# Mixture of experts: expert 0 with 64 unsplit places first, the three fullest other experts split, four more buffers for the first tiles

## The reference

```python
def moe_ffn(h, router_w, w1, w3, w2):
    logits = (h @ router_w).astype(jnp.float32)
    top_vals, top_idx = lax.top_k(logits, TOP_K)          # TOP_K = 2
    top_w = jax.nn.softmax(top_vals, axis=-1)
    gate = jnp.sum(jax.nn.one_hot(top_idx, N_EXPERTS, dtype=jnp.float32) * top_w[..., None], axis=-2)
    out = jnp.zeros_like(h)
    for e in range(N_EXPERTS):
        out = out + gate[..., e:e + 1].astype(h.dtype) * swiglu(h, w1[e], w3[e], w2[e])
    return out
```

## Time and profile before

| | |
|---|---|
| median of 3 runs | 2225.95 us (2222.59 to 2227.03) |
| the profiled execution, its own time | 2226.49 us |
| its span | 2224.7 us |
| TensorE matmul busy | 2108.1 us (95% of the span) |
| TensorE weight load busy | 1787.5 us (80%) |
| VectorE busy | 1347.3 us (61%) |
| ScalarE busy | 1010.9 us (45%) |
| DMA, mean over the span | 220 GB/s, 489.49 MB |
| the 264 expert tiles | issued in two groups of 132, median 13.4 and 14.6 us from issue to landing |

### The profile page before, as it was taken

One profiled execution on the slowest core, in us unless ns is written; L12 is line 12 of the kernel. 1 busy time (PEld: TensorE's weight loads), 2 busy tenths in 40 slices (PEclk: granted clock), 3 DMA queues, 4 the chain that ended last, 5 costly groups with the idle time before them and its releaser, 6 DMA issues. The chain is left out here.

```text
span 2224.7 us, 38921 instructions
## 1 busy us (share of the span) xinstructions
PE 2108.1 (95%) x15459; PEld 1787.5 (80%) x15459; DVE 1347.3 (61%) x2453; ACT 1010.9 (45%) x1759; POOL 124.2 (6%) x115
## 2 busy tenths in 40 slices
PE   8999999999989999989999999889999999998998
PEld 7988889998978888889999888888875568555774
DVE  5565667466668676877666675876941177213942
ACT  5545545546545444456344353455731065113731
POOL 0100000000000050030000041030000000000000
PEclk9999999999999999999999999998999999999999
DMA  6443334444346453354554443356999999999996
GB/s 198 143 136 95 96 114 146 140 140 142 103 123 171 144 155 102 105 179 156 201 194 135 133 152 114 96 171 279 365 361 420 421 420 410 410 420 421 421 396 274
DMA packets 257819, 489.49 MB, mean 220 GB/s; under 512 B 35256, under 2 KB 208216, under 8 KB 223720
## 3 DMA queue, kind: packets, MB, share of 16 engines
q1 hardware_dynamic: 252112, 484.39, 60.4%
q0 software_dynamic: 656, 1.80, 0.2%
q10 hardware_dynamic: 4872, 0.81, 0.2%
HBM read 485.91 MB, written 1.05 MB: 219 GB/s over the span
## 5 line engine op out<-in xcount | busy, mean ns | idle before, releaser
L1336 PE MATMUL bank<-memr 128*128 128x256 f32 (+3 forms) x7056 | 899.7, 287 | 37.6 <-DVE memr L2392 9.6
L1336 PEld LDWEIGHTS bank<-memr 128*128 128x128 f32 (+2 forms) x7056 | 858.4, 186 | 68.9 <-issue 21.0
L2392 DVE TENSOR_TENSOR memr<-mem_low,memr 128x1024 fp32r<-128x1024 f32 (+3 forms) x328 | 398.0, 1232 | 62.9 <-ACT memr L1842 62.2
L1842 ACT CAST memr<-mem_low 128x1024 fp32r<-128x1024 f32 (+3 forms) x328 | 333.3, 1032 | 118.6 <-PE bank L1336 115.6
L1035 ACT ACTIVATE mem_high<-bank 128x128 f32<-128x128 f32 (+1 forms) x88 | 27.9, 317 | 306.2 <-PE bank L854 261.7
L1232 DVE SCALAR_TENSOR_TENSOR mem_high<-mem_high,bank 128x128 f32<-128x128 f32 (+1 forms) x88 | 29.4, 335 | 225.4 <-ACT mem_high L1035 225.4
L847 PE MATMUL bank<-memr 128*128 128x512 f32 x400 | 134.9, 406 | 9.9 <-DVE memr_tail L1178 9.9
L656 PE MATMUL bank<-memr 128*128 128x256 f32 x960 | 117.1, 283 | 3.1 <-DVE memr L2411 3.1
L656 PEld LDWEIGHTS bank<-memr 128*128 128x128 f32 x960 | 115.8, 191 | 3.5 <-issue 3.5
L1178 DVE TENSOR_TENSOR memr_tail<-mem_tail,memr 128x2048 fp32r<-128x2048 f32 x42 | 95.4, 2287 | 32.3 <-ACT memr L1002 31.8
L854 PE MATMUL bank<-mem_ring,mem_low 128*64 128x256 f32 x896 | 102.7, 381 | 1.1 <-DMA mem_ring<-in_moe 1.1
(11 more groups left out here) (357 smaller groups left out, 3018.6 us busy)
## 6 DMA issues: line engine op xcount, KB each, us to landing
mem_tail<-in_moe SPq DMA_DIRECT2D x132, 1024.0 KB, 13.4
mem_ring<-in_moe SPq DMA_DIRECT2D x132, 1024.0 KB, 14.6
mem_low<-in_w_in SPq DMA_DIRECT2D x112, 1024.0 KB, 5.1
mem_tail<-in_ffn_w SPq DMA_DIRECT2D x18, 1024.0 KB, 8.3
mem_low<-in_w_out SPq DMA_DIRECT2D x16, 1024.0 KB, 5.3
mem_low<-in_w_branch SPq DMA_DIRECT2D x12, 1024.0 KB, 5.0
mem_high<-in_ffn_w SPq DMA_DIRECT2D x12, 1024.0 KB, 8.0
mem_low<-in_w_branch SPq DMA_DIRECT2D x16, 512.0 KB, 3.5
```

What stands on the lines that cost most here:

```text
L1336: ins = pe.matmul(out(bank), lhsT, rhs, start=((k, i) == order[0] and not half), stop=((k, i) == order[-1]), skip_group_check=half is not ...
L1842: cp(high, raw).then_inc(*sig("w_high", i))
L2392: st(V.tensor_tensor(low, raw, high, ALU.subtract), sig("w_split", i))
```

## The change

Expert 0 (rank 0) gets 64 places and is not split; ranks 1, 2 and 3 get 128 and are split; ranks 4 to 7 have 64. The order becomes light, light, heavy, light, heavy, light, heavy, light: still three heavy and five light experts. The four high-part buffers are not needed while expert 0 and the next expert run, so they take raw tiles 12 to 15 first; `FIRST` is 16 tiles that can be loaded ahead. TensorE allows these four by a count of `HI` when the router's choice is known, right before the sums that place the tokens. ScalarE's first split waits until tile 15 has been used. Since rank 0 has other room than ranks 1 and 2, up to four passes are possible and VectorE computes the number with four more small operations.

```diff
-ROOMS = [2 * GROUP] * HEAVY + [GROUP] * (EXPERTS - HEAVY)
-TURN = [0, 3, 4, 1, 5, 6, 2, 7]
+ROOMS = [2 * GROUP if 0 < r <= HEAVY else GROUP for r in range(EXPERTS)]
+TURN = [0, 4, 1, 5, 2, 6, 3, 7]
+FIRST = RAW + HI
...
+        raw_hi, hi_r = map(list, zip(*[carve_both(2048) for _ in range(3)]))
+        raw += raw_hi
+        hi_f = [v.bitcast(F32) for v in hi_r]
         hi_f.append(memr_squares[:, 0:2048].bitcast(F32))
         hi_r.append(memr_squares[:, 0:2048])
+        raw.append(sq.rearrange("p a b -> p (a b)")[:, 0:2048])
...
         def tile_done(p, n):

-            return family("m_done"), p * TILES + n + 1 + RAW
+            return family("m_done"), p * (TILES + FIRST) + n + 1 + FIRST
...
+        def slot_of(n):
+
+            return n if n < FIRST else (n - FIRST) % RAW
...
             pe.wait_ge(*at("chosen"))
+            pe.sem_inc(family("m_done"), HI)
...
-                    sp.wait_ge(family("m_done"), p * TILES + n + 1)
+                    if n < FIRST:
+                        sp.wait_ge(family("m_done"), p * (TILES + FIRST) + n + 1)
+                    else:
+                        sp.wait_ge(*tile_done(p, n - (FIRST if n < FIRST + RAW else RAW)))
...
-                if at_ >= HI:
-                    act.wait_ge(*tile_done(p, SPLIT[at_ - HI]))
-                cp(hi_r[at_ % HI], raw[n % RAW]).then_inc(family("m_high"), 1)
+                act.wait_ge(*tile_done(p, SPLIT[at_ - HI] if at_ >= HI else FIRST - 1))
+                cp(hi_r[at_ % HI], raw[slot_of(n)]).then_inc(family("m_high"), 1)
...
+                    if s == 0:
+                        expert_in(p, 0)
                     if s < UPS and heavy(i):
                         high(p, up_tile(s, 0))
                         high(p, up_tile(s, 1))
-                        if s == 0:
-                            expert_in(p, 0)
```

More of the change, by code:

```diff
@@ L63 @@
 TILE_ORDER.update({down_tile(g): (g, 2) for g in range(UPS)})
-SPLIT = [n for n in range(TILES) if TURN[TILE_ORDER[n][0] // HALF] < HEAVY]
+SPLIT = [n for n in range(TILES) if ROOMS[TURN[TILE_ORDER[n][0] // HALF]] > GROUP]
 def constants():
@@ L326, in build @@
         top[0] = 0
-        assert len(raw) == RAW
-        hi_f, hi_r = map(list, zip(*[high_places(2048) for _ in range(3)]))
+        assert len(raw_r) == RAW
+        raw_hi, hi_r = map(list, zip(*[carve_both(2048) for _ in range(3)]))
+        raw += raw_hi
+        hi_f = [v.bitcast(F32) for v in hi_r]
         hi_f.append(memr_squares[:, 0:2048].bitcast(F32))
         hi_r.append(memr_squares[:, 0:2048])
+        raw.append(sq.rearrange("p a b -> p (a b)")[:, 0:2048])
         assert len(hi_r) == HI
@@ L744, in heavy @@
         def heavy(i):
-            return TURN[i] < HEAVY
+            return ROOMS[TURN[i]] > GROUP
         def parts(i):
@@ L754, in heavy_before @@
             return sum(heavy(k) for k in range(i))
+        def slot_of(n):
+            return n if n < FIRST else (n - FIRST) % RAW
         def raw_loaded(p, n):
-            return family(f"m_raw{n % RAW}"), p * (16 * TILES // RAW) + 16 * (n // RAW + 1)
+            k = slot_of(n)
+            if k >= RAW:
+                last = max(range(k - RAW, len(chunks), NSLOT))
+                s, before = at(f"w_loaded{k - RAW}", last)
+                return s, p * 16 + before + 16
+            loads = len(range(k, TILES - FIRST, RAW)) + 1
+            return family(f"m_raw{k}"), p * 16 * loads + 16 * (1 if n < FIRST else (n - FIRST) // RAW + 2)
         def split_done(p, n):
@@ L842, in up @@
                         pe.wait_ge(*split_done(p, n))
-                        high, low = hi_r[SPLIT.index(n) % HI], raw_r[n % RAW]
+                        high, low = hi_r[SPLIT.index(n) % HI], raw_r[slot_of(n)]
                         for k in range(4):
@@ L888, in down @@
                             ins = pe.matmul(SB[0][64 * half:64 * half + 64, :], act_t[:, d % 2, GROUP * f:GROUP * (f + 1)],
-                                            raw[n % RAW][:, f * D + 512 * half:f * D + 512 * half + 512],
+                                            raw[slot_of(n)][:, f * D + 512 * half:f * D + 512 * half + 512],
                                             start=(c == 0 and f == 0), stop=(c == HALF - 1 and f == 1),
@@ L954, in body @@
                 pe.wait_ge(family("m_out_gained"), p * 4 + 4)
+                pe.sem_inc(family("m_done"), FIRST)
             turns(pe, body)
@@ L1158, in moe_dve @@
             st(V.tensor_reduce(most[:, 1:2], over2, AX.X, ALU.max))
+            st(TTn(over3, over2, const("room"), ALU.subtract))
             st(TS(most[:, 2:3], most[:, 0:1], 0.5, 1.0, ALU.is_gt, ALU.add))
@@ L1171, in moe_dve @@
             st.settle()
-            assert PASSES == 3
+            assert PASSES == 4
             def low(p, n):
@@ L1177, in low, with expert_in @@
                 dve.wait_ge(family("m_high"), p * len(SPLIT) + at_ + 1)
-                TTn(raw_r[n % RAW], raw[n % RAW], hi_f[at_ % HI], ALU.subtract).then_inc(family("m_split"), 1)
-            def expert_in(p, i, halves=(0, 1)):
+                TTn(raw_r[slot_of(n)], raw[slot_of(n)], hi_f[at_ % HI], ALU.subtract).then_inc(family("m_split"), 1)
+            def expert_in(p, i):
                 if heavy(i):
-                    for j in halves:
+                    for j in range(2):
                         dve.wait_ge(family("m_he_high"), p * 2 * HEAVY + 2 * heavy_before(i) + j + 1)
```

19 lines of the change are left out of this document (10 added, 9 removed).

## The result

| | before | changed |
|---|---|---|
| median of 5 runs each, side by side | 2227.03 us (2222.59 to 2231.88) | 2211.26 us (2208.24 to 2212.32) |
| ratio | | 0.9929, 95% interval 0.9915 to 0.9943 |
| the profiled execution, its own time; span | 2226.49; 2224.7 us | 2209.96; 2208.1 us |
| TensorE matmul busy | 2108.1 us | 2103.8 us |
| first piece of the opening gather to the last marker | 673.58 us | 658.74 us |

The change is faster by 0.7%, 15.8 us by the medians (13 to 19 by the interval). The forecast was 21.4 us, a median of 2204.6 us.

A forecast was written before the change was run, and what follows sets the result against it. TensorE bounds the heavy experts, losing time between them to late tiles. Start 1541.5 plus eight expert lengths puts the last marker at 2186.8 instead of 2208.15: 21.4 us less, median 2204.6; main range 2201 to 2208, whole 2200 to 2215.

The forecast's parts named there:

- rival A: Stream not ahead at the first heavy expert, extra loads starting only at first tile use: 9.8 us back, 2214.4; chance 0.13.
- a stream without a pause: Sign of being right: DMA at about 420 GB/s without a pause from 1504 to 1700.
- no wait before any heavy expert: Sign of being right: no TensorE idle time over 1 us before any heavy expert's first split product.
- What bounds the kernel: TensorE bounds the heavy experts; a late tile load costs 3.85 us idle plus 1.63 of slow clock, 5.5 us per hole.
- A heavy expert without hole 99.7 us, light after heavy 73.0, light after light 68.8, last light 69.2: Expert lengths from marker to marker; heavy is 105.2 less 5.5, light after light is 72.14 measured less 3.3 of waits.
- The start, 1541.5 and 62.2 us: First product of the expert stage starts at about 1541.5; the first expert, now light, takes 62.2 us.
- I take neither: At the start, up to 1.6 us lost by clock and up to 1.5 us won by a faster 64-column gather, both left out.
- The stream: Four early loads remove the tile stream's pause at 1534.7; it never stops, and the 65th tile lands at 1666.7.
- 2.2 us of room: Before the first heavy expert: its first tile lands at 1666.7 and is needed by 1668.9, the forecast's tightest place.
- Rival B: Splitting, not loading, makes the hole: 5.5 us at each light-to-heavy change, only 4.9 us gained, 2221.1; chance 0.06.
- Rival C: The tile stream becomes the bound: slower under 395 GB/s mean, some 70 us slower at 358 GB/s; chance 0.02.
- Rival D: Expert 0 has more than 64 tokens, so the whole stage runs twice: some 2860 us; chance 0.01.

The follow-up runs named there:

- the two other orders: Changed kernel with light and heavy alternating from expert 0, two light experts adjacent at the end (2215.57 us, 0.9941) or in the middle (2215.64 us, 0.9949).
- the wide gather: Changed kernel with an opening gather of 128 columns instead of 64, the second 64 an unread copy: 2206.28 us (0.9900), again 2209.33 us (0.9915).
- the four loads late: Changed kernel with the four extra loads allowed only when TensorE is about to start its first product: 2215.87 us, 0.9944.
- the one with the seven products: Changed kernel with the 128-column opening gather plus seven unread matmuls, five before the router's choice and two before the gather: 2205.92 us, 0.9905.
- the two kernels kept busy: Changed kernel plus seven unread matmuls before the opening gather's end: with 64 columns 2208.42 us (0.9916), with 128 columns 2205.92 us (0.9905).

## Why the prediction was right, and what it missed

The sign was right, and so was the mechanism of the gain: the hole is a late tile, and the order and the four loads take most of it out. The size was off: 2211.26 us lies inside the whole range of 2200 to 2215, but above the main forecast of 2201 to 2208, in the band 2208 to 2215 to which rival A's 0.13 belonged, and two of its signs of being right (a stream without a pause, no wait before any heavy expert) did not hold. By its own steps:

- *What bounds the kernel.* Right. TensorE bounds the heavy experts, the load is behind the hole and not the split: shown by the two other orders (99.6 us and no wait for a heavy expert behind a single light one, 3.85 us behind a pair).
- *A heavy expert without hole 99.7 us, light after heavy 73.0, light after light 68.8, last light 69.2.* Measured 99.67 and 99.50, 73.08 and 73.09, 68.58, 69.16.
- *The start, 1541.5 and 62.2 us, "I take neither".* Here the two terms were mis-sized, by 3.7 us together. The forecast treated 64 and 128 columns as the same and gave a fall of the clock at most 1.6 us, the price of the old hole. Measured: the clock stayed at half through the whole gather and most of the first product; 0.77 us in the gather, 2.96 us in the first expert. The earlier trace rows had the warning: 0.50 and 0.69 at the old start, too. That the columns are the cause is shown by the wide gather: 62.23 and 62.24 us, the forecast's term; in three traces of it the first product took 3.67 us, in five of the narrow one 6.15 to 6.59.
- *The stream, "so the stream runs on", "it never stops", 2.2 us of room.* This step failed. The four loads did fill the old stop, but the first used buffer came free 11.4 us after the gather's start (1544.25) instead of 8.8 (1543.4), because of the slow first product, with 3.5 us lost, and at the 29th tile the distance of reuse falls from sixteen to twelve tiles, with 2.1 us lost. The second could have been read from the code: the condition in the diff that waits n - FIRST first and n - RAW after. In the first run of the wide gather both dents nearly vanish and the 65th tile is 4.5 us earlier after the gather's start; in the second it is 3.85 us earlier, with 328 and 390 GB/s from 1544 to 1560. Counted from the first load of the stage (1503.14 before, 1501.69 here) the tile was 171.3 - 163.6 = 7.7 us late. The dents explain 5.6 of it, and the rest is a term that the forecast put at nothing: it let the 65th tile land when 65 tiles' bytes had been moved, 68.16 MB. By 1673 the queues had moved 0.97 MB more (the DMA row of the first heavy expert), 2.3 us at 422 GB/s.
- *Rival A* in its mild form happened: "small losses of the stream give anything between". Its full form, the four loads late, came out near its number, 663.4 us where 652.2 + 9.8 = 662.0, but with 3.4 us lost at the start in it, which A had not counted.
- *Rival B* is refuted, by seven split heavy experts without a hole: five in the two other orders, and the second and third of the changed kernel. The one hole that came back there had the landing tile in front of it.
- *Rival C* did not happen: 421 GB/s over the 68 us from 1600, far above its 395. The Trainium skill (DMA: Bandwidth & Descriptors, section Bandwidth) states its share of about 358 GB/s for a core whose neighbour streams too. This program ran on one core, so the condition was not met and the 70 us of the prediction did not follow from it; no row here shows such a share.
- *Rival D*: there was one pass, not two.

Wait, clock and dents add up: 21.4 - 0.8 - 3.0 - 3.1 + 0.3 = 14.8 us in the trace; the medians say 15.8.

The best kernel seen by the traces is the changed one with the opening gather of 128 columns: 0.9900 and 0.9915 of the time before, 654.9 and 654.8 us for the stage (the timed runs do not tell it from the one with the seven products, 0.9905). What remains are 3 to 4 us at the first heavy expert (a wait of 1.7 to 2.3 us and what follows it). To get them the 65th tile has to land earlier, so either loads start earlier in the stage before or another buffer is found; neither was tried.

## What to carry to other kernels

Where a stream feeds two kinds of work, one faster than the stream and one slower, the order decides where its lead is eaten: put two fast pieces together only where the lead is largest, and count the buffers tile by tile at every change of the reuse distance, not only at the first. When a forecast takes out a wait at a phase's start, look up the granted clock there and ask what gives it back; after a pause a wider product can be the faster one. And once one wait is set by a transfer, work won ahead of it goes into the wait, and can lose the clock on top.

## What the runs showed of the hardware

- A gather of 32 float32 products took 7.11 us once and 7.10 us four times with 64 columns, 5.46, 6.66 and 6.71 us with 128 columns, each time begun at a granted clock of about half. With 64 columns the clock stayed at 0.50 to the end of the gather and beyond, with 128 it rose within it. Begun at full clock, after products on nothing, the gather of 128 took about 3.8 us.
- Waits of TensorE for 1.44, 1.45, 1.73, 2.19 and 2.37 us left the granted clock at full level behind them (the product after it took 3.7 us for 32 matmuls, 5.8 for 24), those of 2.30, 2.43, 2.51, 3.27, 3.85 and 3.90 us, and one of 1.50 us, did not. So the length of a wait alone does not decide, and what a hole costs beside its own length varied here from 0 to 2.9 us.
- One core alone loaded at 420 to 424 GB/s beside a busy TensorE, for 68 us in one stretch (1600 to 1668, mostly the second light expert, in six traces: the changed kernel twice, the wide gather twice, and the two kernels kept busy).
- Profiled executions of kernels whose programs are the same up to there reached the opening gather up to 4.8 us apart (1532.74 to 1537.59 us); of one and the same program, 4.6 us apart (1532.83 and 1537.42). What followed repeated to a few tenths.
